# Low-rank and key projections from x times the norm's weight, scaled per token in PSUM

## The chip, the cores and the metric

One core of one Trainium2 chip runs the whole program. The metric is the device time of one execution in microseconds (us); a smaller time is better. TensorE (PE) does the matmuls, VectorE (DVE), ScalarE (ACT) and GpSimd (POOL) the elementwise work, and the DMA queues of SyncE (SP) and POOL move data.

## What is computed

A decoder block on 512 tokens of width 1024, all in float32. The part that the change touches is its beginning: a root-mean-square norm and one wide projection.

```python
def rmsnorm(x, g):
    xf = x.astype(jnp.float32)
    y = xf * lax.rsqrt(jnp.mean(xf * xf, axis=-1, keepdims=True) + NORM_EPS)
    return (y * g.astype(jnp.float32)).astype(x.dtype)
...
        h = rmsnorm(x, norm_mix_g[l])
        proj = h @ w_in[l]
        u_conv, u_rw, gate_logits = jnp.split(
            proj, [COL_CONV, COL_CONV + COL_RKV + COL_LORA], axis=-1)
...
    u = token_shift_lerp(u, mu)
    r, k, v, lw, la, lg = jnp.split(
        u, [RW_WIDTH, 2 * RW_WIDTH, 3 * RW_WIDTH,
            3 * RW_WIDTH + LORA_W, 3 * RW_WIDTH + LORA_W + LORA_A], axis=-1)
```

Of `proj`, the key columns k (512) and the low-rank columns lw, la, lg (160) are used first. Behind them come r, v, the columns of a convolution branch and 2048 gate columns, then a delta-rule recurrence, two output projections, a second norm, and an expert layer over 16384 experts that takes the larger part of the time.

## The kernel before

Channels lie on the 128 partitions and the 512 tokens along the free axis. x is loaded as `xin`, 8 chunks of 128 channels by 512 tokens; h has the same form. Every float32 projection is made of three fp32r matmuls (`mm3`, line 384): each operand is split into a high part (a rounded copy, made by ACT) and a low part (the difference, made by DVE), and high x high, high x low and low x high are summed in a PSUM bank. So h has the tiles `hH` and `hL`, a weight block has `wH` and `wL`, and the low-rank weights have `wloH` and `wloL`.

The weights of the wide projection come as blocks of 128 output channels, w0, w1 and so on. Blocks w0 to w3 give the keys, w4 to w7 r, w8 to w11 v. A block is 8 chunks x 3 = 24 matmuls of 512 columns. Raw blocks lie in four buffers (`wraw`), split ones in only two (`wH`, `wL`): block n+2 can be split when the matmuls of block n are done. ACT makes the high part in `split_h(n)` (line 1025), DVE the low part in `split_l(n)` (line 1467), and PE waits for `wl_ready` before a block.

Each engine runs a program of its own in the order written; semaphores join them. The order of the start is, on each engine:

- ACT: squares of the 8 chunks of x; the high part of the low-rank weights (line 1042); the square root of the norm (line 1045, tile `rs`); w0 and w1 split; the 8 high parts of h; then `lora_a` and `lora_b` out of PSUM, scaled (line 1056), a tanh and a sigmoid on them, and for each block its scaled copy out of PSUM into `k_in` (line 1097) and `split_h(n + 2)`.
- DVE: the sum of the squares (`grow_sum`), the low part of the low-rank weights, the reciprocal of `rs` (line 1493), then in one loop h and its low part chunk by chunk (lines 1495 to 1500), `split_l(0)`, `split_l(1)`, the token shift of both low-rank results and of each block (`lerp`, line 1505), each block's followed by `split_l(n + 2)`.
- PE: the mean of the squares over channels (`mean_square`, line 403, one float32 matmul with a matrix of 1/1024, called ms1), the low-rank projection `lora_a` (64 outputs) and `lora_b` (96 outputs), 24 matmuls each, then `units_free()` (line 376), which waits until the banks 0 to 5 are free, and blocks w0 to w11 in turn.

A bank is handed over by two semaphores: PE raises `filled`, and the last reader raises `taken`. Blocks w0, w1, ... use the banks 6 and 7 in turn, so block n waits for block n-2 to be taken.

## Time and profile before

| | us |
|---|---|
| median of 3 runs | 1812.72 |
| lowest to highest | 1811.16 to 1813.22 |
| the profiled execution | 1812.87 |
| its span in the trace | 1810.9 |

The span is what the trace covers, from the first to the last instruction; the profiled execution took 2.0 us more than that. PE is busy for 96% of the span. The stretch in which it isn't is the start, and the change lies there. The timeline, which lists instructions with their start and length in order of time, is the view to read, together with the bracket behind a row, which tells how long the engine had been idle and who ended it.

### The profile page before, as it was taken

To read this page: it belongs to the slowest core of one execution; us is meant where nothing else is said; L and a number is where in the kernel's file an instruction comes from. 1 tells how busy PE (TensorE), PEld (TensorE's weight loads), DVE (VectorE), ACT (ScalarE), POOL (GpSimd) and SP (SyncE) were. 2 spreads that over 40 slices of the span, in tenths; PEclk is the share of its full clock that TensorE was granted. 3 is DMA by queue.
4 is the path that set the end of the run, shared out by engine and by line. 5 is a ranking of instruction groups with operands and counts; after the bars stand their busy time and mean duration, and the time that the engine had idled before them with its cause. 6 is when DMAs were issued, how large, how long until landed. Compare 5 with 4: busy or idle time off the path is not lost.

```text
span 1810.9 us, 33740 instructions
## 1 busy us (share of the span) xinstructions
PE 1745.3 (96%) x11997; PEld 1542.4 (85%) x11997; DVE 1421.2 (78%) x2759; ACT 737.1 (41%) x1049; POOL 593.5 (33%) x532
## 2 busy tenths in 40 slices
PE   5989999999979999999999899999999999999998
PEld 3878888877858799999999888888888888888887
DVE  5377777846479999979998588888888888888886
ACT  4464544352232233347777233333333333333333
POOL 0000000002000166678886344443333433334430
PEclk9999999989989999999999999999999999999999
DMA  4221121116222144456666999999999999999992
GB/s 162 82 71 37 49 77 55 54 66 243 94 75 77 69 160 159 159 175 251 223 223 228 352 377 367 367 361 349 336 330 343 343 348 348 347 361 339 336 335 84
DMA packets 157823, 399.06 MB, mean 220 GB/s; under 512 B 12432, under 2 KB 78096, under 8 KB 155696
## 3 DMA queue, kind: packets, MB, share of 16 engines
q1 hardware_dynamic: 118032, 252.20, 39.8%
q0 software_dynamic: 39712, 145.77, 21.5%
q8 instruction: 54, 0.88, 0.2%
q14 instruction: 25, 0.20, 0.0%
HBM read 353.88 MB, written 44.04 MB: 220 GB/s over the span
## 4 chain that ended last, share of the span: by engine, by line
PE 54%; issue 15%; POOL 4%; DMA 2%; DVE 1%; SPq 1%; ACT 0%; POOLq 0%; ACTq 0%; DVEq 0%
PE unit L382 54%; POOL uL L2105 4%; DMA vraw<-v_tab 1%; SPq L928 0%; DMA g_dram<-ge 0%; DMA sgw<-gate_dram 0%; DVE yo L2069 0%; SPq L941 0%; DVE accs L2006 0%; ACT vH L1011 0%; DVE aL L1981 0%; DVE mb L1836 0%; DVE uL L1945 0%; DVE wL L1471 0%; ACT sqj L1011 0%
## 5 line engine op out<-in xcount | busy, mean ns | idle before, releaser
L382 PE MATMUL unit<-h2H,uH 128*128 128x384 f32 x1024 | 355.8, 347 | 11.3 <-POOL uL L2105 9.1
L382 PE MATMUL unit<-h2H,uL 128*128 128x384 f32 x1024 | 344.9, 337 | 0.0
L382 PE MATMUL unit<-h2L,uH 128*128 128x384 f32 x1024 | 344.5, 336 | 0.0
L2133 POOL DMA_INDIRECT ring<-u_tab,idx x128 | 170.7, 1333 | 230.2 <-DVE accs L2006 198.1
L382 PE MATMUL unit<-vH,aH 128*128 128x512 f32 x768 | 238.6, 392 | 5.1 <-DVE vL L1987 5.1
L382 PE MATMUL unit<-vL,aH 128*128 128x512 f32 x768 | 237.7, 391 | 0.0
L382 PE MATMUL unit<-vH,aL 128*128 128x512 f32 x768 | 237.6, 391 | 0.0
L1987 DVE TENSOR_TENSOR vL<-vraw,vH 128x1024 fp32r<-128x1024 f32 x128 | 156.6, 1224 | 88.9 <-ACT vH L1011 88.5
L2133 POOL DMA_INDIRECT ring<-v_tab,idx x128 | 141.1, 1102 | 241.0 <-DVE ring L1992 238.3
L1011 ACT ACTIVATE aH<-af 128x384 fp32r<-128x384 f32 x128 | 67.0, 524 | 366.1 <-DVE af L1976 366.1
L382 PEld LDWEIGHTS unit<-h2H,uH 128*128 128x128 f32 x1024 | 193.9, 189 | 21.5 <-POOL uL L2105 16.1
L382 PEld LDWEIGHTS unit<-h2L,uH 128*128 128x128 f32 x1024 | 193.8, 189 | 2.4
L382 PEld LDWEIGHTS unit<-h2H,uL 128*128 128x128 f32 x1024 | 193.3, 189 | 0.0
L2105 POOL TENSOR_TENSOR uL<-uraw,uH 128x1024 fp32r<-128x1024 f32 x40 | 112.0, 2801 | 191.0 <-ACT uH L1011 191.0
L1011 ACT ACTIVATE ge<-unit 128x384 f32<-128x384 f32 x128 | 62.0, 484 | 269.7 <-PE unit L382 264.4
L382 PEld LDWEIGHTS unit<-vL,aH 128*128 128x128 f32 x768 | 144.7, 188 | 31.3
L382 PEld LDWEIGHTS unit<-vH,aL 128*128 128x128 f32 x768 | 144.4, 188 | 30.8
L382 PEld LDWEIGHTS unit<-vH,aH 128*128 128x128 f32 x768 | 143.7, 188 | 31.3 <-DVE vL L1987 5.4
L2006 DVE SCALAR_TENSOR_TENSOR accs<-ring,spa,accs 128x1024 f32<-128x1024 f32 x128 | 164.2, 1283 | 4.7 <-DVE spa L1997 3.3
L2122 POOL TENSOR_SCALAR oh<-cst,e2s 128x128 f32<-128x128 f32 x192 | 148.7, 787 | 30.2 <-PE unit L382 27.7
L1992 DVE SCALAR_TENSOR_TENSOR ring<-ring,h2T 128x1024 f32<-128x1024 f32 x128 | 156.2, 1220 | 0.0
L2078 POOL DMA_DIRECT2D gate_dram<-gst x16 | 8.9, 554 | 402.9 <-ACT gst L1011 402.9
(298 smaller groups left out, 3411.4 us busy)
## 6 DMA issues: line engine op xcount, KB each, us to landing
uraw<-uT SPq DMA_DIRECT2D x128, 512.0 KB, 7.6
vraw<-v_tab SPq DMA_DIRECT2D x128, 512.0 KB
wraw<-wall SPq DMA_DIRECT2D x68, 512.0 KB, 3.7
w_dram<-wst SPq DMA_DIRECT2D x12, 2048.0 KB, 6.7
wg<-w_dram SPq DMA_DIRECT2D x32, 768.0 KB
g_dram<-ge SPq DMA_DIRECT2D x64, 192.0 KB, 1.9
gl<-g_dram SPq DMA_DIRECT2D x32, 384.0 KB
gate_dram<-gst POOLq DMA_DIRECT2D x16, 256.0 KB, 2.4
```

The lines of the kernel that those rows point to most:

```text
L382: return pe.matmul(out, lhsT, rhs, start=start, stop=stop, skip_group_check=True)
L1011: return act.activation(out, in_, f, **kw)
L1987: tt(vL[:, g, :], vraw[:, g, :], vH[:, g, :], ALU.subtract).then_inc(vl_dve, 1)
L1992: stt(ring[k][:, :], ring[k][:, :], 1.0, h2T[:, :], ALU.mult, ALU.mult, accum_out=spd[:, k:k + 1]).then_inc(row_used, 1)
L2006: stt(accs[:, :], ring[k][:, :], spa[:, k:k + 1], accs[:, :], ALU.mult, ALU.add).then_inc(row_used, 1)
L2078: pool.dma_start(gate_dram[k], gst[:, k % 2, :]).then_inc(gate_stored[k % 2], 16)
L2105: pool.tensor_tensor(uL[:, slot % 2, :, :], uraw[:, slot, :, :], uH[:, slot % 2, :, :], ALU.subtract).then_inc(ul_ready, 1)
L2122: ins = pool.tensor_scalar(oh2[:, b, k, :], C(C_IOTA), e2s[:, tok:tok + 1], None, ALU.is_equal)
L2133: pool.indirect_dma_start(out=ring[k][:, :], out_offset=None, in_=(u_tab, v_tab)[half], in_offset=bass.IndirectOffsetOnAxis(ap=idx[:, SR * ...
```

## The change

Since the norm divides a token's whole column by one number, h @ W is (x * g) @ W scaled per token. For the low-rank columns and the key blocks w0 to w3 the kernel now multiplies with `xa` = x * g and scales the result in PSUM:

- `xa` gets a high part `xaH` (ACT, a copy of `xin` scaled by the weight) and a low part `xaL` (DVE), in memory of their own. They come first on both engines, with the split of the low-rank weights behind the fifth chunk. The squares, their sum and the splits of w0 and w1 come after that.
- PE begins with the low-rank matmuls, now chunk by chunk for both outputs, then makes ms1, and then w0 to w3 from `xa`. w2 and w3 use the banks 3 and 4. `units_free()` comes behind w3, and w4 and all later blocks use h as before.
- A new DVE instruction `scale_back` multiplies a result in PSUM by `rs`. There are six: both low-rank results behind the fourth chunk of the loop that makes h, w0 behind that loop, and w1 to w3 each behind the token shift of the block ahead of it. ACT's scaled copies wait for them (`scaled`).
- `split_h(2)` and `split_l(2)` move into the loop that makes h, behind its sixth chunk; the later ones stay behind their blocks.
- On the SP queue the vectors come first, then x, the low-rank weights, `cst`, w0, and only then the other constants and w1 to w3.

```diff
@@ -119,2 +119,4 @@
     xin = at("xin", 159, [P, DC, T])
+    xaH = [at(f"xaH{k}", o, [P, DC // 2, T], F32R) for k, o in enumerate((81, 60))]
+    xaL = at("xaL", 191, [P, DC, T], F32R)
     hH = at("hH", 93, [P, DC, T], F32R)
@@ -278,3 +280,4 @@
                                           ["cst_loaded", "lora_loaded", "small_loaded", "keys_loaded"])
-        s_x = [sem(f"x{i}_loaded") for i in range(2)]
+        s_x, s_vec = [sem(f"x{i}_loaded") for i in range(2)], sem("vec_loaded")
+        xa_high, xa_split, scaled = sem("xa_high"), sem("xa_split"), sem("scaled")
         sum_grown = sem("sum_grown")
@@ -413,3 +416,14 @@
                 for c in range(DC // 2):
+                    if n == CB:
+                        pe.wait_ge(h_split, c + 1)
                     mm3(o[:, :], wH[:, n % WSPL, c, :], wL[:, n % WSPL, c, :], hH[:, c, :], hL[:, c, :], c == 0, False)
+            def key_block(n):
+                o = begin(f"w{n}", 6 - 3 * (n // 2) + n % 2)
+                pe.wait_ge(wl_ready, n + 1)
+                for c in range(DC):
+                    last = mm3(o[:, :], wH[:, n % WSPL, c, :], wL[:, n % WSPL, c, :],
+                               xaH[c // 4][:, c % 4, :], xaL[:, c, :], c == 0, c == DC - 1)
+                last.then_inc(fill_sem(f"w{n}"), 1)
@@ -418,2 +432,4 @@
                 for c in range(DC // 2, DC):
+                    if n == CB:
+                        pe.wait_ge(h_split, c + 1)
                     last = mm3(o[:, :], wH[:, n % WSPL, c, :], wL[:, n % WSPL, c, :], hH[:, c, :], hL[:, c, :],
@@ -427,14 +443,16 @@
-            pe.wait_ge(s_cst, 80)
+            pe.wait_ge(wlol_ready, 1)
+            lora = [(name, begin(name, b), lo, n) for name, b, lo, n in
+                    (("lora_a", 1, 0, LW + LA), ("lora_b", 2, LW + LA, LG))]
+            for c in range(DC):
+                pe.wait_ge(xa_split, c + 1)
+                for name, o, lo, n in lora:
+                    last = mm3(o[0:n, :], wloH[:, c, lo:lo + n], wloL[:, c, lo:lo + n],
+                               xaH[c // 4][:, c % 4, :], xaL[:, c, :], c == 0, c == DC - 1)
+                    if c == DC - 1:
+                        last.then_inc(fill_sem(name), 1)
+            pe.wait_ge(s_cst, 64)
             mean_square("ms1", 0, rs, 0)
-            pe.wait_ge(wlol_ready, 1)
-            for name, b, lo, n in (("lora_a", 1, 0, LW + LA), ("lora_b", 2, LW + LA, LG)):
-                o = begin(name, b)
-                for c in range(DC):
-                    pe.wait_ge(h_split, c + 1)
-                    last = mm3(o[0:n, :], wloH[:, c, lo:lo + n], wloL[:, c, lo:lo + n], hH[:, c, :], hL[:, c, :],
-                               c == 0, c == DC - 1)
-                last.then_inc(fill_sem(name), 1)
+            for n in range(CB):
+                key_block(n)
@@ -661,3 +679,3 @@
             pe.wait_ge(s_small, 32)
-            for n in range(W_CONV):
+            for n in range(CB, W_CONV):
                 if n == 5:
@@ -905,2 +923,3 @@
         def _(sp):
+            sp.dma_start(vec[:, :], vecs).then_inc(s_vec, 16)
             for i in range(2):
@@ -908,3 +927,5 @@
                 sp.dma_start(xin[:, half, :], xT[:, half, :]).then_inc(s_x[i], 16)
+            sp.dma_start(wlo[:, :, :], wlora).then_inc(s_lora, 16)
             sp.dma_start(cst[:, :, :], consts).then_inc(s_cst, 16)
+            sp.dma_start(wraw[:, 0, :, :], wall[0]).then_inc(w_loaded[0], 16)
             sp.dma_start(sml[:, :, :], smalls).then_inc(s_cst, 16)
@@ -912,5 +933,3 @@
             sp.dma_start(rst[:, :], reset).then_inc(s_cst, 16)
-            sp.dma_start(vec[:, :], vecs).then_inc(s_cst, 16)
-            sp.dma_start(wlo[:, :, :], wlora).then_inc(s_lora, 16)
-            for s in range(WRAW):
+            for s in range(1, WRAW):
                 sp.dma_start(wraw[:, s, :, :], wall[s]).then_inc(w_loaded[s], 16)
@@ -1034,2 +1053,3 @@
+            act.wait_ge(s_vec, 16)
             for c in range(DC):
@@ -1037,2 +1057,9 @@
                     act.wait_ge(s_x[c // (DC // 2)], 16)
+                fn(xaH[c // 4][:, c % 4, :], xin[:, c, :], ACT.Copy, scale=vc("gmix", c)).then_inc(xa_high, 1)
+                if c == DC // 2:
+                    act.wait_ge(s_lora, 16)
+                    fn(wloH[:, :, :], wlo[:, :, :], ACT.Copy).then_inc(wloh_ready, 1)
+            for c in range(DC):
+                if c == 2:
+                    split_h(0)
                 if c >= 2:
@@ -1040,10 +1067,8 @@
                 fn(sq[:, c % 2, :], xin[:, c, :], ACT.Square).then_inc(sq_ready, 1)
-            act.wait_ge(s_lora, 16)
-            fn(wloH[:, :, :], wlo[:, :, :], ACT.Copy).then_inc(wloh_ready, 1)
+            split_h(1)
             wait_filled(act, "ms1")
-            act.wait_ge(s_cst, 80)
             root(rs[:, :], "ms1", 0).then_inc(take_sem("ms1"), 1)
-            split_h(0)
-            split_h(1)
             for c in range(DC):
+                if c == 6:
+                    split_h(2)
                 act.wait_ge(h_new, c + 1)
@@ -1053,4 +1078,4 @@
-            for name, dst, n, col in (("lora_a", lwa, LW + LA, 12), ("lora_b", lgs, LG, 13)):
-                wait_filled(act, name)
+            for k, (name, dst, n, col) in enumerate((("lora_a", lwa, LW + LA, 12), ("lora_b", lgs, LG, 13))):
+                act.wait_ge(scaled, k + 1)
                 fn(dst[0:n, :], ps(name)[0:n, :], ACT.Copy, scale=omu[0:n, col:col + 1]).then_inc(lora_part, 1)
@@ -1094,6 +1119,10 @@
             for n in range(W_CONV):
-                wait_filled(act, f"w{n}")
+                if n < CB:
+                    act.wait_ge(scaled, n + 3)
+                else:
+                    wait_filled(act, f"w{n}")
                 dst = {"k": k_in, "r": r_in, "v": v_in}[KRV[n // CB]]
                 fn(dst[:, n % CB, :], ps(f"w{n}")[:, :], ACT.Copy, scale=omu[:, n:n + 1]).then_inc(lerp_part, 1)
-                split_h(n + 2)
+                if n:
+                    split_h(n + 2)
                 if n == 3:
@@ -1483,13 +1512,28 @@
+            dve.wait_ge(s_vec, 16)
+            tick(tsc(omka[:, :], vc("ka", 0, CB), -1.0, 1.0, ALU.mult, ALU.add))
+            tick(tsc(omu[:, :], vc("mu", 0, 14), -1.0, 1.0, ALU.mult, ALU.add))
+            for c in range(DC):
+                dve.wait_ge(xa_high, c + 1)
+                stt(xaL[:, c, :], xin[:, c, :], vc("gmix", c), xaH[c // 4][:, c % 4, :], ALU.mult, ALU.subtract
+                    ).then_inc(xa_split, 1)
+                if c == DC // 2:
+                    dve.wait_ge(wloh_ready, 1)
+                    tt(wloL[:, :, :], wlo[:, :, :], wloH[:, :, :], ALU.subtract).then_inc(wlol_ready, 1)
             for c in range(DC):
                 grow_sum(0, rs, sq, c)
-            dve.wait_ge(s_cst, 80)
-            tick(tsc(omka[:, :], vc("ka", 0, CB), -1.0, 1.0, ALU.mult, ALU.add))
-            tick(tsc(omu[:, :], vc("mu", 0, 14), -1.0, 1.0, ALU.mult, ALU.add))
-            dve.wait_ge(wloh_ready, 1)
-            tt(wloL[:, :, :], wlo[:, :, :], wloH[:, :, :], ALU.subtract).then_inc(wlol_ready, 1)
+                if c == 4:
+                    split_l(0)
+            split_l(1)
             wait_taken(dve, "ms1")
-            tick(dve.reciprocal(rs[:, :], rs[:, :]))
+            rs_ready = tick(dve.reciprocal(rs[:, :], rs[:, :]))
             after()
+            def scale_back(name, n):
+                wait_filled(dve, name)
+                after(rs_ready)
+                tt(ps(name)[0:n, :], ps(name)[0:n, :], rs[0:n, :], ALU.mult).then_inc(scaled, 1)
             for c in range(DC + 1):
@@ -1500,5 +1544,8 @@
                     tt(hL[:, c - 1, :], h[:, c - 1, :], hH[:, c - 1, :], ALU.subtract).then_inc(h_split, 1)
-            split_l(0)
-            split_l(1)
+                if c == 3:
+                    scale_back("lora_a", LW + LA)
+                    scale_back("lora_b", LG)
+                elif c == 6:
+                    split_l(2)
+            scale_back("w0", P)
@@ -1562,3 +1609,6 @@
                 lerp(f"w{n}", dst[:, n % CB, :], P, vc("mu", n), lerp_part, n + 1, take_sem(f"w{n}"))
-                split_l(n + 2)
+                if n:
+                    split_l(n + 2)
+                if n + 1 < CB:
+                    scale_back(f"w{n + 1}", P)
                 if n == 4:
```

PE at the start. In these rows `unit` is the PSUM bank, `rs,cst` is ms1, `xaH_73` and `xaH_74` are the two halves of `xaH`. Before:

```order
L382 MATMUL unit<-rs,cst 128x512 [waits sum_grown,cst_loaded]
L382 MATMUL unit<-hH,wloH 64x512 [waits h_split,wlol_ready]
...
L382 MATMUL unit<-hH,wH 128x512 [waits small_loaded,bank2_taken,wl_ready,bank1_taken,bank0_taken]
L382 MATMUL unit<-hL,wH 128x512
L382 MATMUL unit<-hH,wL 128x512
```

and now:

```order
L385 MATMUL unit<-xaH_73,wloH 64x512 [waits xa_split,wlol_ready]
...
L385 MATMUL unit<-rs,cst 128x512 [waits sum_grown,cst_loaded]
L385 MATMUL unit<-xaH_73,wH 128x512 [waits wl_ready]
...
L385 MATMUL unit<-hH,wH 128x512 [waits small_loaded,bank4_taken,bank6_taken,bank3_taken,wl_ready,bank2_taken,h_split,bank1_taken,bank0_taken]
```

ms1 has moved from the front to behind the 48 low-rank matmuls, and the wait for banks 0 to 5 from w0 to w4, where it now takes in w2 and w3 too.

DVE behind the reciprocal of the norm: the end of the loop that makes h, and what follows until the fourth block is split. Before:

```order
L1497 SCALAR_TENSOR_TENSOR h<-xin,vec,rs 128x512
L1500 TENSOR_TENSOR hL<-h,hH 128x512 [waits h_high] x2
L1471 TENSOR_TENSOR wL<-wraw,wH 128x1024 [waits wh_ready] x2
L1508 SCALAR_TENSOR_TENSOR lwa<-unit,vec,lwa 64x511 [waits lora_part]
L1508 SCALAR_TENSOR_TENSOR lgs<-unit,vec,lgs 96x511 [waits lora_part]
L1508 SCALAR_TENSOR_TENSOR k_in<-unit,vec,k_in 128x511 [waits lerp_part]
L1471 TENSOR_TENSOR wL<-wraw,wH 128x1024 [waits wh_ready]
L1508 SCALAR_TENSOR_TENSOR k_in<-unit,vec,k_in 128x511 [waits lerp_part]
```

and now:

```order
L1500 TENSOR_TENSOR wL<-wraw,wH 128x1024 [waits wh_ready]
L1541 SCALAR_TENSOR_TENSOR h<-xin,vec,rs 128x512
L1544 TENSOR_TENSOR hL<-h,hH 128x512 [waits h_high] x2
L1537 TENSOR_TENSOR unit<-unit,rs 128x512 [waits dve_order,bank6_filled]
L1555 SCALAR_TENSOR_TENSOR lwa<-unit,vec,lwa 64x511 [waits lora_part]
L1555 SCALAR_TENSOR_TENSOR lgs<-unit,vec,lgs 96x511 [waits lora_part]
L1555 SCALAR_TENSOR_TENSOR k_in<-unit,vec,k_in 128x511 [waits lerp_part]
L1537 TENSOR_TENSOR unit<-unit,rs 128x512 [waits dve_order,bank7_filled]
L1555 SCALAR_TENSOR_TENSOR k_in<-unit,vec,k_in 128x511 [waits lerp_part]
L1500 TENSOR_TENSOR wL<-wraw,wH 128x1024 [waits wh_ready]
```

The first `wL` row of the new order is `split_l(2)`, inside the loop; the last is `split_l(3)`, behind two token shifts of keys and the scaling of w0 and w1.

ACT in the same place, the high parts of h (`hH`), the low-rank results (`lwa`, `lgs`), the keys (`k_in`) and the splits (`wH`). Before:

```order
L1011 ACTIVATE hH<-h 128x512 [waits h_new] x8
L1011 ACTIVATE lwa<-unit,omu 64x512 [waits bank1_filled,zero_ready]
L1011 ACTIVATE lgs<-unit,omu 96x512 [waits bank2_filled]
L1011 ACT_TABLE_LOAD
L1011 ACTIVATE lwa<-lwa 32x512 [waits bank1_taken]
L1011 ACT_TABLE_LOAD
L1011 ACTIVATE lgs<-lgs 96x512 [waits bank2_taken]
L1011 ACTIVATE k_in<-unit,omu 128x512 [waits bank6_filled]
L1011 ACTIVATE wH<-wraw 128x1024 [waits bank6_filled,w2_loaded]
```

and now:

```order
L1030 ACTIVATE wH<-wraw 128x1024 [waits bank6_filled,w2_loaded]
L1030 ACTIVATE hH<-h 128x512 [waits h_new] x2
L1030 ACTIVATE lwa<-unit,omu 64x512 [waits scaled,zero_ready]
L1030 ACTIVATE lgs<-unit,omu 96x512 [waits scaled]
L1030 ACT_TABLE_LOAD
L1030 ACTIVATE lwa<-lwa 32x512 [waits bank1_taken]
L1030 ACT_TABLE_LOAD
L1030 ACTIVATE lgs<-lgs 96x512 [waits bank2_taken]
L1030 ACTIVATE k_in<-unit,omu 128x512 [waits scaled] x2
L1030 ACTIVATE wH<-wraw 128x1024 [waits bank7_filled,w3_loaded]
```

The split of w2 has moved ahead of the last two high parts of h; that of w3, the last row, stands behind both copies of keys and both table loads.

## Rows read from the trace of the kernel before

**Rows 1.** Stretches (us): length, busy PE, PEld, DVE, ACT, POOL, PE clock, DMA share, GB/s.
```profile
0.00:10.00 10.00, 0.00 (x0) 0.00 (x0) 2.94 (x6) 4.64 (x7) 0.19 (x4) 1.00 0.81 306
60.30:1810.90 1750.60, 1707.02 (x11852) 1515.99 (x11850) 1390.77 (x2720) 710.63 (x1015) 593.31 (x528) 0.98 0.62 223
```

**Rows 2.** Timeline, PE: start, length, out<-in, count, idle before and releaser.
```profile
12.95 2.05 PE L382 MATMUL unit<-rs,cst 128*128 128x512 f32 x2 [12.95 <-DVE rs L1480]
22.03 0.66 PE L382 MATMUL unit<-hH,wloH 128*64 128x512 f32 x1 [7.03 <-DVE hL L1500]
...
28.03 0.42 PE L382 MATMUL unit<-hH,wloL 128*64 128x512 f32 x1
...
36.37 0.40 PE L382 MATMUL unit<-hH,wloL 128*96 128x512 f32 x1
...
38.48 0.47 PE L382 MATMUL unit<-hH,wH 128*128 128x512 f32 x1 [1.71 <-issue]
...
60.33 0.39 PE L382 MATMUL unit<-hH,wH 128*128 128x512 f32 x1
```

**Rows 3.** Timeline, ACT and DVE up to the reciprocal's end.
```profile
6.14 1.75 ACT L1011 ACTIVATE sq<-xin 128x512 f32<-128x512 f32 x3 [4.12 <-DMA xin<-xT]
...
13.05 1.27 ACT L1011 ACTIVATE wloH<-wlo 128x1280 fp32r<-128x1280 f32 x1 [1.18 <-DMA wlo<-wlora]
...
14.35 1.49 DVE L1490 TENSOR_TENSOR wloL<-wlo,wloH 128x1280 fp32r<-128x1280 f32 x1 [1.39 <-ACT wloH L1011]
15.63 0.69 ACT L1011 ACTIVATE rs<-unit,vec 128x512 f32<-128x512 f32 x1
...
16.35 3.35 DVE L1493 RECIPROCAL rs<-rs 128x512 f32<-128x512 f32 x1 [0.51 <-ACT rs L1011]
```

**Rows 4.** Groups by line, 0 to 500 us: float32 matmuls of 512 columns, busy us, mean ns.
```profile
L382 PE MATMUL unit<-cy,cst 128*128 128x512 f32 x8 | 3.7, 605 | 0.0
```

**Rows 5.** Timeline, DVE and ACT: the loop that makes h, and the splits behind it.
```profile
19.74 1.42 DVE L1497 SCALAR_TENSOR_TENSOR h<-xin,vec,rs 128x512 f32<-128x512 f32 x2
...
28.11 0.75 DVE L1497 SCALAR_TENSOR_TENSOR h<-xin,vec,rs 128x512 f32<-128x512 f32 x1
...
28.90 0.63 ACT L1011 ACTIVATE hH<-h 128x512 fp32r<-128x512 f32 x1 [0.63 <-DVE h L1497]
...
30.17 2.35 DVE L1471 TENSOR_TENSOR wL<-wraw,wH 128x1024 fp32r<-128x1024 f32 x2
```

**Rows 6.** Timeline, DVE: an operation that reads PSUM.
```profile
115.22 0.68 DVE L1615 TENSOR_TENSOR lt<-unit,sml 128x512 f32<-128x512 f32 x1
```

**Rows 7.** Timeline, ACT and DVE: low-rank results, first keys, split of w2.
```profile
36.81 0.68 ACT L1011 ACTIVATE lgs<-unit,omu 96x512 f32<-96x512 f32 x1 [4.82 <-PE unit L382]
37.51 1.28 ACT L1011 ACT_TABLE_LOAD   x1
...
40.75 0.63 ACT L1011 ACTIVATE lgs<-lgs 96x512 f32<-96x512 f32 x1
44.20 0.69 ACT L1011 ACTIVATE k_in<-unit,omu 128x512 f32<-128x512 f32 x1 [2.83 <-PE unit L382]
...
45.88 1.23 DVE L1471 TENSOR_TENSOR wL<-wraw,wH 128x1024 fp32r<-128x1024 f32 x1 [0.20 <-ACT wH L1011]
```

**Rows 8.** Timeline, PE: small matmuls of the key norms, then block w5.
```profile
65.77 3.86 PE L382 MATMUL unit<-sel,sqk 128*128 128x8 f32 x32
69.48 0.77 PE L382 MATMUL unit<-hH,wH 128*128 128x512 f32 x1
...
72.54 0.39 PE L382 MATMUL unit<-hL,wH 128*128 128x512 f32 x1
```

**Rows 9.** Stretches of 2 us around them, columns as in rows 1.
```profile
70.00:72.00 2.00, 2.00 (x6) 1.56 (x5) 0.00 (x0) 0.00 (x0) 0.00 (x0) 0.50 0.80 258
```

**Rows 10.** Timeline, PE and ACT: the next wait of PE, and the work that leads to it.
```profile
119.26 1.28 ACT L1011 ACT_TABLE_LOAD   x1 [5.82 <-PE unit L382]
...
135.10 1.13 PE L382 MATMUL unit<-bh,nkt 64*64 64x64 f32 x32 [4.58 <-DVE r_in L1555]
```

## The prediction

> **What bounds the kernel now.** I read the stretches first. Behind 60.3 us PE is busy for 1707.0 of 1750.6 us [rows 1], so whatever moves the start of that part moves the end. It begins with block w4, at 60.33 [rows 2], and from w4 on the change leaves every instruction as it was. The question is therefore one number: when does w4 start? The timeline of PE shows what precedes it now. PE is idle up to 12.95, makes ms1, is idle 7.03 us more until the first chunk of h is split at 22.03, does the low-rank matmuls until about 36.8, waits 1.71 us for their banks, and then runs w0 to w3 without a gap from 38.48 [rows 2]. So some 22 us of the first 38 are waits for the norm and for h. The change lets PE begin without the norm. What then matters is the chain on ACT and DVE that the norm still feeds, because w2, w3 and w4 hang on it.
>
> Two prices of a matmul of 512 columns serve throughout. At full speed it is (60.33 - 38.48) / 96 = 0.228 us [rows 2]. From 22.03 to 28.03 fourteen of them took 6.0 us, 0.43 each [rows 2]: half speed, after a long idle stretch. The same is seen behind the small matmuls of the key norms: from 69.48 to 72.54 seven took 3.06 us [rows 8], with a granted clock of 0.50, the 1.2 GHz level [rows 9]. So a cold start costs 6.0 - 14 x 0.228 = 2.8 us in the one case and 3.06 - 7 x 0.228 = 1.5 us in the other.
>
> **Part 1: when PE starts.** Now the low-rank weights land at 13.05, when their split begins [rows 3]. About 1.0 MB (cst, two small tables and the reset mask) goes behind them in the queue; at 306 GB/s with the DMA engines 0.81 busy, thus up to 378 [rows 1], that is 2.6 to 3.3 us earlier, less 0.3 for the 0.1 MB of vectors put in front of x: 10.1 to 10.7. ACT has x at 6.14 [rows 3], now 6.4; its table load of 1.28 us waits for x in the new order, and five copies at about 0.6 (three squares took 1.75 [rows 3]) end at 10.7. So transfer and copies arrive together. The split of these weights takes 1.30 us to the start of its low part and 1.49 more [rows 3]: ready at 13.5, PE starts at 13.7. All `xaL` chunks are there in time: PE takes six matmuls a chunk, 1.4 us at the least, DVE 0.7.
>
> Low-rank: 48 x 0.228 = 10.9 us plus a cold start of 1.5 to 2.8, of which I take 2.1: end at 26.7 (26.1 to 27.4). The sum of squares and the splits of w0 and w1 on ACT and DVE, 8 squares, 8 sums and four splits, are done by 25, in the cover of this; if they were later, ms1 would be later by as much. ms1 is a float32 matmul: 3.7 us for 8 pieces [rows 4], two pieces here, about 1.0 at full speed (2.05 now [rows 2]). Filled at 27.8. w0 and w1 follow at 27.7 and end at 38.6.
>
> **Part 2: the split of w2.** The square root starts at 27.9. From its start to the first chunk of h is 19.74 - 15.63 = 4.11 us [rows 3, 5], so h begins at 32.0. The loop reaches the place of `split_l(2)` after 28.11 - 19.74 = 8.37 us [rows 5], plus two `scale_back` of the low-rank results. No row has that operation; an operation of the same size that reads PSUM takes 0.68 [rows 6]. Writing PSUM too could cost nothing or as much again; I take 0.6 each, since they overlap a little. `split_l(2)` starts at 41.6 and takes 1.2 [rows 5]: w2 can start at 42.9. **PE idles 4.3 us** behind w1.
>
> **Part 3: the split of w3.** This is the long wait. Behind `split_l(2)` the last h chunk starts at 42.75; its high part starts 0.79 later and takes 0.63 [rows 5], so ACT is free at 44.2. Then, in order: the copy of `lora_a` 0.65, and from the start of the copy of `lora_b` to the end of the sigmoid 40.75 + 0.63 - 36.81 = 4.57 [rows 7], with two table loads in it: 49.4. Copy of w0's keys, 0.73 until DVE can take it (as from root to reciprocal, 16.35 - 15.63 [rows 3]): 50.1. Token shift of w0 and `scale_back` of w1, 0.65 each: 51.5 with the handover. Then as now from a key copy to the low part of the next block, 45.88 - 44.20 = 1.68, and 1.23 for it [rows 7]: 54.4. w3 starts at 54.6. w2 has ended between 48.4 and 51.2, at full speed or cold, and that difference is hidden. **PE idles 3.4 to 6.2 us.**
>
> **Part 4: w4.** w3 needs 24 x 0.228 = 5.45 us plus a cold start p of 0 to 2.8. `units_free()` now waits for w3: `scale_back` 0.1 + 0.7, copy 0.73, token shift 0.75, handover 0.2 make 2.5 us. w4 starts at 54.6 + 5.45 + 2.5 + p = 62.5 + p. For p I take 1.4: a wait of this length has both outcomes near it (1.71 us idle at 36.8 left the speed as it was [rows 2]; the 4.58 at 130.5 and what led up to it stand for the other side [rows 10]), and 1.5 is the smaller of the two cold starts.
>
> **Sum.** 63.9 against 60.33, thus 3.6 us later. What it saves, the start at 13.7 instead of 22.03, is given back in three waits of 4.3, 3.4 to 6.2 and 2.5 us. The profiled execution took 1812.87, its span plus 2.0, and the median is 1812.72: 1812.7 + 3.6 = 1816.3. Everything later shifts by the same amount. I checked the first wait behind w4 for slack: PE idles 4.58 us up to 135.10, but the ACT work that leads to it itself waited 5.82 us for PE at 119.26 [rows 10], so it moves along.
>
> A rule of the skill speaks against the change. The two table loads, which the new order puts on PE's path, take 1.28 us with nothing behind them: from the first load's start to the sigmoid is 3.24 us, two loads and the tanh [rows 7]. The Trainium skill, page ScalarE: Activation LUTs, section What ACT_TABLE_LOAD costs, puts a drain of about 1.38 us on top of each switch. By that rule the sum would be about 2.8 us more, estimated from that page; the rows have no room for it.
>
> **The rivals.**
>
> (a) *A kind clock, not slower.* The low-rank matmuls start warm after a short stretch (1.5), w2's lateness leaves PE idle so briefly that w3 starts at full speed (p = 0), and the slow stretch behind the key norms [rows 8] falls elsewhere, a gain of up to 1.5. From 63.9: -0.6 - 1.4 - 1.5, thus w4's start in effect at 60.4 and 1812.8. It decides at p: with p under 0.5 and a short cold start the change is level. For it: the 1.71 us wait cost nothing. Against: both waits are twice that and more.
>
> (b) *An unkind clock, slower.* The long cold start (2.8), p = 2.8, and one more short cold start at w4 behind its wait of 2.5: +0.7 + 1.4 + 1.5 on the sum, 1819.9.
>
> (c) *Slack behind w4.* If the waits behind it were for work that the new order finishes earlier (the low-rank results), 3.6 us would be taken up in part: 1812.7 to 1815. Against it stands [rows 10].
>
> (d) *The chain is dearer than its rows.* `scale_back` in PSUM at twice the price, six of them with four on the path (+2.7), or table loads with a pause behind them: 1819 to 1821. The table-load rule above gives 1819.1 as its own result; I give that 3%.
>
> (e) *The change does not do what it says*: PE does not start before 22, because the low-rank weights land late. Then ms1 is 8 us later and so is all behind it: 1824. Only a queue that ignores its order could do that.
>
> **How the numbers follow.** The sum as worked out, 1814.5 to 1818.5, has 0.58; (a) 0.14; (b) 0.12; (c) 0.06; (d) 0.08; (e) 0.02. The likeliest case gives 1816.3. The range reaches from inside (a) to (b) and the start of (d): 1812.5 to 1820.5. Of this kernel 0.2%, or 3.6 us, is about what can be told from no change. The forecast lies on that line: half of the main case is above it, with (b), (d), (e), which makes 0.50 slower; 0.47 within; 0.03 faster, since nothing that I see takes w4 3.6 us ahead of 60.33. The Trainium skill, page TensorE: Matmul & The Clock Gate, Part 1, says that the number of slow matmuls at a start differs from run to run of one kernel; no run here shows that yet, and it would be a reason for a spread of the size of (a) and (b).
>
> **What would show each step right or wrong.** The first low-rank matmul near 13.7 (part 1); ms1 behind them near 26.7; the first matmul of w2 near 42.9 with 4.3 us of idle time, released by DVE's `wL` (part 2); the first of w3 near 54.6, also released by `wL` (part 3); w4 near 64 with about 2.5 us idle (part 4); the length of w3 tells p. Behind w4 the stretches should be as before, 1750.6 us. The prediction is wrong if w2 or w3 starts without a wait, or if the part behind w4 changes its length by more than 1.5 us.

## The result

| | before | changed |
|---|---|---|
| median, 14 runs each | 1810.16 us | 1815.77 us |
| the profiled execution of the changed kernel | | 1817.64 us, span 1815.7 |
| ratio of the times, changed to before | | 1.0028, 95% interval 1.0020 to 1.0037 |

The change makes the kernel slower by 0.28%, about 5.1 us; 3.6 us were forecast, and a time inside 1812.5 to 1820.5 us. One of the 14 runs of the changed kernel took 1952.60 us at a mean granted clock of 0.842; it isn't in the ratio, and the median of the other 13 is 1815.38 us.

Where the time is, is told by one cut. Stretches of the changed kernel, from the start to w4 and from w4 to the end (columns as in [rows 1]):

```profile
0.00:65.65 65.65, 40.56 (x146) 29.28 (x147) 40.33 (x55) 32.79 (x45) 0.19 (x4) 0.92 0.39 136
65.65:1815.70 1750.05, 1707.45 (x11851) 1515.20 (x11851) 1390.73 (x2719) 708.82 (x1013) 593.87 (x528) 0.99 0.62 223
```

Behind w4 it is 1750.05 us, 1750.60 before [rows 1]. So in these two traces the whole difference lies ahead of w4, which starts at 65.65 instead of 60.33: 5.3 us, and the medians differ by about as much.

The timeline of PE shows the shape (as [rows 2]; `xaH,wH` are blocks from xa, `hH,wH` is w4):

```profile
14.12 0.69 PE L385 MATMUL unit<-xaH,wloH 128*64 128x512 f32 x1 [14.12 <-DVE wloL L1522]
...
18.44 0.63 PE L385 MATMUL unit<-xaL,wloH 128*96 128x512 f32 x1
18.87 0.48 PE L385 MATMUL unit<-xaH,wloL 128*96 128x512 f32 x1
...
27.50 1.02 PE L385 MATMUL unit<-rs,cst 128*128 128x512 f32 x2
...
43.52 0.79 PE L385 MATMUL unit<-xaH,wH 128*128 128x512 f32 x1 [4.09 <-DVE wL L1500]
...
50.19 0.39 PE L385 MATMUL unit<-xaH,wL 128*128 128x512 f32 x1
54.77 0.80 PE L385 MATMUL unit<-xaH,wH 128*128 128x512 f32 x1 [4.19 <-DVE wL L1500]
55.36 0.63 PE L385 MATMUL unit<-xaL,wH 128*128 128x512 f32 x1
...
62.57 0.39 PE L385 MATMUL unit<-xaH,wL 128*128 128x512 f32 x1
65.65 0.47 PE L385 MATMUL unit<-hH,wH 128*128 128x512 f32 x1 [2.70 <-issue]
```

The first low-rank matmul starts 7.9 us earlier than before (14.12 for 22.03). Behind that PE idles three times: 4.09 us for the low part of w2, 4.19 for that of w3, 2.70 at the banks ahead of w4. The lengths tell the second half of the loss: matmuls of 0.63 us are at half speed, those of 0.39 at full speed (the next one starts 0.43 and 0.23 us later). w3 goes from 54.77 to 62.8, 8.0 us for 5.45. The clock in stretches of 2 us within w4 falls as well:

```profile
66.00:68.00 2.00, 2.00 (x8) 1.60 (x7) 0.62 (x1) 1.81 (x3) 0.00 (x0) 0.71 0.20 37
68.00:70.00 2.00, 2.00 (x6) 1.52 (x6) 0.00 (x0) 0.00 (x0) 0.00 (x0) 0.50 0.60 225
```

w4 ran for 7.2 us, though its first matmuls were at full speed: the granted clock fell to 0.50, the 1.2 GHz level, after PE had begun again.

Why w3 is so late is read on ACT and DVE (compare [rows 7]):

```profile
44.70 0.67 ACT L1030 ACTIVATE lwa<-unit,omu 64x512 f32<-64x512 f32 x1
45.27 0.67 ACT L1030 ACTIVATE lgs<-unit,omu 96x512 f32<-96x512 f32 x1
45.95 1.28 ACT L1030 ACT_TABLE_LOAD   x1
47.25 0.63 ACT L1030 ACTIVATE lwa<-lwa 32x512 f32<-32x512 f32 x1
47.90 1.28 ACT L1030 ACT_TABLE_LOAD   x1
49.19 0.63 ACT L1030 ACTIVATE lgs<-lgs 96x512 f32<-96x512 f32 x1
49.73 0.67 ACT L1030 ACTIVATE k_in<-unit,omu 128x512 f32<-128x512 f32 x1
```

```profile
45.43 0.69 DVE L1537 TENSOR_TENSOR unit<-unit,rs 128x512 f32<-128x512 f32 x1
46.03 0.73 DVE L1555 SCALAR_TENSOR_TENSOR lwa<-unit,vec,lwa 64x511 f32<-64x511 f32 x1
46.69 0.73 DVE L1555 SCALAR_TENSOR_TENSOR lgs<-unit,vec,lgs 96x511 f32<-96x511 f32 x1
50.43 0.75 DVE L1555 SCALAR_TENSOR_TENSOR k_in<-unit,vec,k_in 128x511 f32<-128x511 f32 x1 [3.01 <-ACT k_in L1030]
51.10 0.69 DVE L1537 TENSOR_TENSOR unit<-unit,rs 128x512 f32<-128x512 f32 x1
52.54 0.75 DVE L1555 SCALAR_TENSOR_TENSOR k_in<-unit,vec,k_in 128x511 f32<-128x511 f32 x1 [0.75 <-ACT k_in L1030]
53.49 1.23 DVE L1500 TENSOR_TENSOR wL<-wraw,wH 128x1024 fp32r<-128x1024 f32 x1 [0.20 <-ACT wH L1030]
```

w0's keys were scaled in PSUM from 46.1 on (first DVE row), but ACT copies them at 49.73, behind the tanh, the sigmoid and two table loads. DVE waits 3.01 us for that. Only then come w1's keys, and behind them the split of w3, at PE's disposal from 54.7.

### The profile page after: what moved, and what is told of

Same layout as the page of the kernel before. It is cut to its first block, busy times and chain, and to the rows that moved or that the text cites. A ratio compares the mean times of both kernels' runs of the same rounds, so it can differ in the third digit from the quotient of the medians.

```text
span 1815.7 us, 33768 instructions
## 1 busy us (share of the span) xinstructions
PE 1748.0 (96%) x11997; PEld 1544.5 (85%) x11997; DVE 1431.1 (79%) x2773; ACT 741.6 (41%) x1057; POOL 594.1 (33%) x532
## 4 chain that ended last, share of the span: by engine, by line
PE 54%; issue 15%; POOL 4%; DMA 2%; DVE 1%; SPq 1%; ACT 0%; POOLq 0%; ACTq 0%; DVEq 0%
PE unit L385 54%; POOL uL L2155 4%; DMA vraw<-v_tab 1%; SPq L947 0%; DMA g_dram<-ge 0%; DMA sgw<-gate_dram 0%; DVE yo L2119 0%; SPq L960 0%; DVE accs L2056 0%; ACT vH L1030 0%; DVE aL L2031 0%; DVE mb L1886 0%; DVE uL L1995 0%; DVE wL L1500 0%; ACT sqj L1030 0%
## 5 line engine op out<-in xcount | busy, mean ns | idle before, releaser
L2183 POOL DMA_INDIRECT ring<-u_tab,idx x128 | 174.6, 1364 | 225.2 <-DVE accs L2056 192.4
```

The lines of the kernel that those rows point to most:

```text
L2183: pool.indirect_dma_start(out=ring[k][:, :], out_offset=None, in_=(u_tab, v_tab)[half], in_offset=bass.IndirectOffsetOnAxis(ap=idx[:, SR * ...
```

## The experiments

The theory: the time follows the start of w4, and that start is set by a chain (ms1, root, h, ACT's queue, splits, banks) plus PE's clock. Each of the first four kernels is the changed kernel with one link of it taken out. One table holds them all; "w4" is the start of its first matmul in the trace, "behind w4" the rest of the span, the ratio is to the kernel before on the same chip, and the last column is the ratio's distance from 1, times 1810.

| kernel | w4 | behind w4 | ratio (95% interval) | us against before |
|---|---|---|---|---|
| before | 60.33 | 1750.6 | | |
| changed | 65.65 | 1750.0 | 1.0028 (1.0020 to 1.0037) | +5.1 |
| e1, banks waited for later | 59.49 | 1748.1 | 1.0003 (0.9992 to 1.0014) | +0.5 |
| e2, tanh and sigmoid later | 58.49 | 1748.8 | 1.0009 (0.9995 to 1.0023) | +1.6 |
| e3, matmuls of no use in the waits | 64.33 | 1746.9 | 1.0015 (1.0002 to 1.0028) | +2.7 |
| e4, ms1 earlier | 60.23 | 1746.5 | 1.0010 (1.0000 to 1.0020) | +1.8 |
| e5, low-rank part alone | 68.45 | 1749.2 | 1.0051 (1.0036 to 1.0066) | +9.2 |
| e6, own tiles for w2 and w3 | 60.81 | 1750.2 | 1.0023 (1.0013 to 1.0034) | +4.2 |
| c1 = e1 + e2 + e4 | 54.10 | 1749.7 | 0.9954 (0.9940 to 0.9967) | -8.3 |
| c2 = c1 + e6 | 49.76 | 1749.2 | 0.9950 (0.9937 to 0.9964) | -9.1 |

Two things limit what this table can tell. First, "less than the changed kernel" below is a difference of two ratios, each with its interval; put together (the half-widths added in squares, an estimate) they leave 2.4 to 3.1 us on either side. Second, w4 is read from one execution, and that one lies up to 3.7 us from its kernel's median: 2.7 us above it for the kernel before (1812.87 against 1810.16), 2.3 above for the changed one (1817.64 against 1815.38), 2.0 below for e2, 3.7 below for e4. The time against before and the shift of w4 agree to within 4 us in all nine kernels, with the largest gaps at e6 (3.7) and e2 (3.4); so the theory holds in the main and is not shown to better than that.

### e1: the wait for the banks

```diff
-            units_free()
             pe.wait_ge(s_small, 32)
             for n in range(CB, W_CONV):
                 if n == 5:
+                    units_free()
                     key_norms()
```

> The changed kernel, with the wait for banks 0 to 5 moved from ahead of w4 to ahead of the key norms, the first that needs them; w4 itself uses bank 6. Theory (the time follows the start of w4 and its clock): in the changed kernel PE idles 2.70 us from the end of w3 (62.8) to w4 (65.65), and w4 is then partly at half speed, 7.2 us long for 5.45. Now w4 starts near 62.9, warm: 2.8 + 1.7 = 4.5 us less than the changed kernel, which is level with the kernel before within 1 us. Rival (what follows w4, its key norms and the low-rank work, waits for the same ACT and DVE work anyway): w4 starts early, but the key norms start at 72.8 as they do now, and nothing is gained.

Measured: 4.5 us less than the changed kernel by the ratios (2.0 to 7.0 with both intervals), level with before. w4 follows w3 without a gap:

```profile
53.92 0.50 PE L385 MATMUL unit<-xaH,wH 128*128 128x512 f32 x1 [2.69 <-DVE wL L1500]
...
59.27 0.39 PE L385 MATMUL unit<-xaH,wL 128*128 128x512 f32 x1
59.49 0.39 PE L385 MATMUL unit<-hH,wH 128*128 128x512 f32 x1
...
64.94 3.63 PE L385 MATMUL unit<-sel,sqk 128*128 128x8 f32 x32
```

The key norms start at 64.94, not at 72.8, so the rival falls. The gain is the one expected, but in the trace w4 starts even 6.2 us earlier, and not all of that is the edit's. The edit gives 2.9 us; the start of the trace (w0 at 27.12, not 27.96) gives 0.8. And in this trace w2 ran cold for longer (13 slow matmuls for 6), which cost nothing since w3 was not yet split, but made the idle time ahead of w3 2.69 us instead of 4.19, and w3 ran at full speed, 2.6 us less. That part is the clock, not the edit.

### e2: tanh and sigmoid off ACT's way

```diff
-            wait_taken(act, "lora_a")
-            fn(lwa[0:LW, :], lwa[0:LW, :], ACT.Tanh).then_inc(lora_ready, 1)
-            wait_taken(act, "lora_b")
-            fn(lgs[:, :], lgs[:, :], ACT.Sigmoid).then_inc(lora_ready, 1)
...
+                elif n == 4:
+                    wait_taken(act, "lora_a")
+                    fn(lwa[0:LW, :], lwa[0:LW, :], ACT.Tanh).then_inc(lora_ready, 1)
+                    wait_taken(act, "lora_b")
+                    fn(lgs[:, :], lgs[:, :], ACT.Sigmoid).then_inc(lora_ready, 1)
                 elif n == 5:
```

> The changed kernel, with the tanh and the sigmoid of the low-rank results (and their two table loads) moved on ACT behind block w4's copy; they are first needed at w6. Theory (the split of w3 hangs on ACT's queue): ACT can copy w0's keys at 46.2 instead of 49.7, DVE then sets the pace with two token shifts of the low-rank results, the low part of w3 ends at 51.7 instead of 54.7, w3 starts near 51.8 after an idle time of 1.3 us and so at full speed, and w4 starts near 59.9 instead of 65.65: 5.8 to 7.5 us less than the changed kernel, 1 to 2 us less than before. Rival (DVE's own work, scaling in PSUM above all, holds the chain): w3 moves by less than 1 us and the time by less than 1.5.

ACT and DVE in this kernel:

```profile
43.67 0.67 ACT L1030 ACTIVATE lgs<-unit,omu 96x512 f32<-96x512 f32 x1
44.56 0.69 ACT L1030 ACTIVATE k_in<-unit,omu 128x512 f32<-128x512 f32 x1 [0.22 <-DVE unit L1538]
```

```profile
48.80 1.23 DVE L1501 TENSOR_TENSOR wL<-wraw,wH 128x1024 fp32r<-128x1024 f32 x1 [0.20 <-ACT wH L1030]
```

and PE, the first matmuls of w3 and w4:

```profile
50.08 0.50 PE L385 MATMUL unit<-xaH,wH 128*128 128x512 f32 x1
...
58.49 0.47 PE L385 MATMUL unit<-hH,wH 128*128 128x512 f32 x1 [2.67 <-issue]
```

From the copy of `lora_b` to the keys of w0 it is 0.9 us instead of 4.5, and the low part of w3 is ready at 50.0, 8.1 us behind the start of w2 (41.92) where it took 11.2. w3 follows w2 without a wait (w2 itself had eleven slow matmuls), w4 starts at 58.49, after much the same wait at the banks (2.67). In the trace w4 is 7.2 us earlier, but 1.6 us of that are there before any of the edit acts: ms1 starts at 25.92, not 27.50, since PE began 0.6 us sooner and six matmuls were slow at the start instead of eleven. By the ratios the gain on the changed kernel is 3.4 us (0.4 to 6.4), less than the 5.8 expected. The chain is as the theory says; how much of it reaches the time is less certain, since its interval reaches from -0.9 to +4.2 us against before and the forecast of 1 to 2 us faster lies at or beyond its lower end. The rival falls by its first half, since w3 starts 4.7 us earlier where it allowed 1; its gain of less than 1.5 us is not excluded by the times.

### e3: keeping PE busy in its waits

```diff
+            def keep_busy(k):
+                for _ in range(k):
+                    mm(bank[5][:, :], xaH[0][:, 0, 0:P], xaH[0][:, 0, :])
+
             for n in range(CB):
+                if n >= 2:
+                    keep_busy((16, 16)[n - 2])
                 key_block(n)
+            keep_busy(8)
```

> The changed kernel, with matmuls of no use (xa with itself, into bank 5, which nobody reads) in PE's waits: 16 ahead of w2, 16 ahead of w3, 8 behind w3. Starts of w2 and w3 should stay at 43.5 and 54.8, as ACT and DVE set them. Theory (cold starts cost 2.6 us in w3 and 1.7 in w4): w3 takes 5.5 us instead of 8.0, w4 starts near 63.1 and takes 5.5 instead of 7.2: 4.3 us less than the changed kernel, 0.5 to 1 over before. Rival (the clock would have paid its slow stretch later anyway, at the key norms, as it did in the kernel before): w4 starts at 63.1 but the gain at the end is 2.5 us or less.

```profile
54.26 0.51 PE L385 MATMUL unit<-xaH,wH 128*128 128x512 f32 x1 [1.85 <-DVE wL L1507]
...
55.31 0.51 PE L385 MATMUL unit<-xaL,wH 128*128 128x512 f32 x1
55.62 0.63 PE L385 MATMUL unit<-xaH,wL 128*128 128x512 f32 x1
```

w2 began at full speed, at 43.01. The 16 matmuls ahead of w3 ended at 52.4, 1.85 us too early, and w3 started fast but then fell to half speed for seven matmuls. w4 was at full speed. So w4 starts 1.3 us earlier, and the ratios differ by 2.4 us, half of what was expected and not clear of no gain at all (-0.4 to 5.2). The kernel did not keep w3 at full speed, so it is no clean test of what the cold starts cost; both theories stay open. In the trace w4 took 5.5 us instead of 7.2, but this kernel paid more behind the key norms: there eleven matmuls ran slowly, in the changed kernel and in the kernel before seven. An idle time of 1.7 us left the clock as it was in the kernel before [rows 2], one of 1.85 us was followed by a fall here.

### e4: ms1 earlier

```diff
             for c in range(DC):
+                if c == 5:
+                    pe.wait_ge(s_cst, 64)
+                    mean_square("ms1", 0, rs, 0)
                 pe.wait_ge(xa_split, c + 1)
...
-            pe.wait_ge(s_cst, 64)
-            mean_square("ms1", 0, rs, 0)
```

> The changed kernel, with the mean of the squares (ms1) moved on PE from behind the eighth chunk of the low-rank matmuls to ahead of the sixth: the sum of squares is there at 22.9, the sixth chunk starts at 23.3, the place of ms1 in the changed kernel is 27.5. Theory (everything from the root on is a chain behind ms1): root at 24.4 instead of 28.6, w2 at 39.5 right behind w1, w3 at 50.7 after 5.7 us idle and cold, w4 near 61.3: 4 us less than the changed kernel, about 1 over before. Rival (the chain is held by ACT and DVE work that does not hang on ms1): the root is 4 us earlier but w3 moves by less than 2.

```profile
24.28 0.69 ACT L1031 ACTIVATE rs<-unit,vec 128x512 f32<-128x512 f32 x1 [0.43 <-PE unit L385]
```

```profile
39.24 0.50 PE L385 MATMUL unit<-xaH,wH 128*128 128x512 f32 x1
...
50.49 0.80 PE L385 MATMUL unit<-xaH,wH 128*128 128x512 f32 x1 [5.51 <-DVE wL L1501]
60.23 0.76 PE L385 MATMUL unit<-hH,wH 128*128 128x512 f32 x1 [2.67 <-issue]
```

Root at 24.28, w2 right behind w1, w3 at 50.49 after 5.51 us idle: each within 0.3 us of what was written down. w4 is 1.1 us earlier than expected, since w3 was slow for six matmuls only, and the time 3.3 us below that of the changed kernel (0.9 to 5.7). The rival falls: w3 moved by 4.3 us.

PE's order is only the smaller part of the norm's lateness. The root starts at 24.28 here, and at 15.63 in the kernel before [rows 3]. These 8.7 us are left to ACT and DVE, where the splits of xa, of the low-rank weights and of w0 stand ahead of or among the squares and their sum. In the changed kernel the last three sums are:

```profile
20.63 2.28 DVE L1509 TENSOR_TENSOR rs<-rs,sq 128x512 f32<-128x512 f32 x3
```

so the sum is there at 22.9, where ms1 could start at 12.95 before [rows 2]. No kernel here makes the squares first, so what that order would give, and what it would cost at PE's start, is not known.

### e5: the low-rank part alone

```diff
-            for n in range(CB):
-                key_block(n)
...
-            for n in range(CB, W_CONV):
+            for n in range(W_CONV):
...
-                    act.wait_ge(scaled, n + 3)
+                wait_filled(act, f"w{n}")
...
-                if n + 1 < CB:
-                    scale_back(f"w{n + 1}", P)
```

(and `split_h(2)`, `split_l(2)` back behind w0, `scale_back("w0", P)` gone.)

> The changed kernel with its key part undone: only the low-rank columns are made from xa and scaled in PSUM; w0 to w3 are made from h, in the banks 6 and 7, with their splits behind them, as in the kernel before. Theory (the norm is late because ms1 stands behind the low-rank matmuls, and everything that needs h waits for it): the loop that makes h still ends near 44.3, the low-rank results are taken near 46.3, w0 starts near 46.5, cold after some 18 us idle, and w4 near 70 against 65.65 in the changed kernel: 3 to 4 us slower than that, 8 to 9 slower than before. Rival (the key part, with its four scalings and its late splits, is what costs): it is faster than the changed kernel.

```profile
45.02 0.76 PE L385 MATMUL unit<-hH,wH 128*128 128x512 f32 x1 [17.36 <-DVE lwa L1544]
...
68.45 0.39 PE L385 MATMUL unit<-hH,wH 128*128 128x512 f32 x1
```

PE waits 17.36 us for h and the low-rank results; w4 starts 2.8 us later than in the changed kernel, and the time is 4.2 us above it (1.1 to 7.3). This kernel ran only four times, within 1819.28 to 1821.18 us. So the key part is not what costs: it wins back a part of what the late norm takes. The loss comes with the low-rank part, which puts work ahead of the norm, on PE ahead of ms1 (e4) and on ACT and DVE ahead of the squares.

### e6: tiles of their own for the splits of w2 and w3

```diff
+    wX = {2: (at("w2H", 44, [P, DC, P], F32R), at("w2L", 48, [P, DC, P], F32R)),
+          3: (at("w3H", 181, [P, DC, P], F32R), at("w3L", 185, [P, DC, P], F32R))}
...
-                if c == 6:
+                if c == 3:
                     split_h(2)
+                elif c == 5:
+                    split_h(3)
...
-                elif c == 6:
+                elif c == 4:
                     split_l(2)
+                elif c == 6:
+                    split_l(3)
...
-                if n:
-                    split_h(n + 2)
+                if n in (1, 2):
+                    split_h(n + 3)
+                elif n >= 4:
+                    split_h(n + 2)
```

> The changed kernel, with tiles of their own for the split weights of w2 and w3, in memory that is free at that time, so that both can be split inside the loop that makes h; the splits of w4 and w5 move forward to behind w1 and w2. Theory: w0 to w3 run without a gap from 28.5 to 50.3; but w4 still waits until w3 is scaled, copied and shifted, and that hangs on ACT's queue with the tanh and the sigmoid: w4 near 62, cold, against 65.65. So the two long waits turn into one of 11 us, and only 3.5 us are gained on the changed kernel, 1.5 slower than before. Rival (the late splits are the whole loss): w4 near 53 and 10 us gained.

```profile
39.88 0.50 PE L393 MATMUL unit<-xaH,w2H 128*128 128x512 f32 x1 [1.56 <-DVE w2L L1514]
60.81 0.77 PE L393 MATMUL unit<-hH,wH 128*128 128x512 f32 x1 [9.75 <-issue]
```

```profile
49.22 0.63 ACT L1038 ACTIVATE lgs<-lgs 96x512 f32<-96x512 f32 x1
49.76 0.67 ACT L1038 ACTIVATE k_in<-unit,omu 128x512 f32<-128x512 f32 x1
```

The two waits for splits shrink to 1.56 us (none was expected), and one of 9.75 stands ahead of w4. ACT comes to the keys of w0 at 49.76, as in the changed kernel (49.73), and three more blocks of keys have to be scaled, copied and shifted behind it. The time is only 0.9 us below that of the changed kernel by the ratios (-1.5 to 3.3), less than the 3.5 expected and not clear of no gain, where the trace has w4 4.8 us earlier. Slow matmuls explain little of that gap: nine in w4 and seven behind the key norms, where the changed kernel had seven and seven. Of the 4.8 us, 1.1 were there at ms1 (26.40 for 27.50), and the two traces lie 1.2 us below and 2.3 us above their kernels' medians. The rest stays open. Late splits are thus not the whole loss; they are one of two ends of the same chain.

### c1 and c2: the edits together

> Three of the single edits together: the wait for the banks at the key norms, tanh and sigmoid behind w4's copy, ms1 ahead of the sixth low-rank chunk. Theory (their gains lie one behind the other on one chain and add up, less what the cold starts take): root 24.4, w2 at 39.4, w3 near 47.5, w4 right behind it near 53 against 60.33 in the kernel before: 7 us faster than before, ratio 0.996. Rival (the gains overlap): w4 at 57 or later, 3 us or less.

> The same three edits, and the early splits of w2 and w3 as well. Theory: PE runs from 13.9 to the key norms without a wait, w4 starts at 49.5 to 50, 10.5 us ahead of the kernel before, and the key norms start near 55.3: 10 to 11 us faster than before, ratio 0.994, and 15 faster than the changed kernel. Rival (the stages behind w4 then wait for ACT and DVE, which have not been freed by as much): half of it.

```profile
22.63 1.10 PE L385 MATMUL unit<-rs,cst 128*128 128x512 f32 x2 [0.22 <-DVE rs L1511]
...
46.91 0.50 PE L385 MATMUL unit<-xaH,wH 128*128 128x512 f32 x1 [2.37 <-DVE wL L1502]
...
54.10 0.39 PE L385 MATMUL unit<-hH,wH 128*128 128x512 f32 x1
```

That is c1: behind ms1 one wait is left, 2.37 us for w3, with seven slow matmuls in that block. In c2 it is gone too:

```profile
13.96 0.69 PE L393 MATMUL unit<-xaH,wloH 128*64 128x512 f32 x1 [13.96 <-DVE wloL L1538]
...
49.76 0.39 PE L393 MATMUL unit<-hH,wH 128*128 128x512 f32 x1
...
55.73 2.48 PE L393 MATMUL unit<-sel,sqk 128*128 128x8 f32 x21 [0.38 <-ACT sqk L1039]
```

Both are faster than the kernel before and the changed one: c1 by 0.46%, c2 by 0.50%, against 0.4 and 0.6 expected. The gains of e1, e2 and e4 do add up within what can be told: 4.5, 3.4 and 3.3 make 11.2 us, and c1 is 13.4 us below the changed kernel. From c1 to c2 w4 starts 4.3 us earlier in the traces, but the times differ by less than their intervals, so the forecast of 10 to 11 us for c2 is neither reached nor excluded (9.1, interval 6.5 to 11.4); c2 is the fastest by its median, 1801.73 us, without c1 being shown slower.

## The prediction, step by step

The forecast was 3.6 us slower; it is 5.1. The time itself came closer, 1816.3 forecast and 1815.77 measured, but that is luck: the forecast added its 3.6 to a median of three runs, 1812.72, and 14 runs of the same kernel have 1810.16. By its own steps, in the trace of the changed kernel:

| step | predicted | measured |
|---|---|---|
| PE starts | 13.7 | 14.12 |
| ms1 starts | 26.7 | 27.50 |
| root, first chunk of h | 27.9, 32.0 | 28.56, 32.67 |
| w2 starts, idle before | 42.9, 4.3 | 43.52, 4.09 |
| sigmoid ends | 49.4 | 49.8 |
| w3 starts, idle before | 54.6, 3.4 to 6.2 | 54.77, 4.19 |
| cold start in w3 (p) | 1.4 | 2.6 |
| w4 starts, idle before | 63.9, 2.5 | 65.65, 2.70 |
| behind w4 | 1750.6 | 1750.0 |

**Part 1 held**, 0.4 us late, since x was there at 6.9, not 6.4 (timeline of ACT):

```profile
6.91 1.28 ACT L1030 ACT_TABLE_LOAD   x1 [6.91 <-DMA xin<-xT]
```

The low-rank matmuls had eleven at half speed, so a cold start of 2.2 us where 2.1 was taken, and 0.2 us more went into their pitch. **Part 2 held**: `scale_back`, for which no row stood, takes 0.68 to 0.70 us with 0.6 from one to the next, as the row that reads PSUM did [rows 6]; writing PSUM as well costs nothing that can be seen. **Part 3 held**: from the root to w3 it is 26.2 us, 26.7 were summed, because its delays were rows of the same instructions. **Part 4 is where the size was off**: p was taken as 1.4 and was 8.03 - 5.46 = 2.6 us, eleven slow matmuls and the parts of one at either end. That is inside its bounds of 0 to 2.8, and the row leaned on, 1.71 us idle without effect, was too short a wait to tell of one of 4.19.

Rival (a), the kind clock, would have needed p under 0.5. Rival (b) foresaw cold starts in w3 and in w4, and both came: w4 was slow for seven matmuls, 1.7 us. It still did not come to 7 us, since the stretch behind w4, with that loss in it, is no longer than before. From the end of w4 on it is even 2.2 us shorter (1742.9 for 1745.1), and 1.8 of this is in the small matmuls of the convolution's variance, 32 of one column, in the kernel before and in the changed one:

```profile
374.62 5.57 PE L382 MATMUL unit<-cst,csq 128*128 128x1 f32 x32
```

```profile
380.55 3.73 PE L385 MATMUL unit<-cst,csq 128*128 128x1 f32 x32
```

The granted clock was 0.65 over the first (374.62 to 380.05) and 1.00 over the second (380.55 to 384.14). The change can't be what made it: these 32 took 3.73 us in the traces of changed, e1, e3 and e4, and 5.38 to 5.57 in the other six. So 1.8 us of luck in this one place hid what w4's cold start cost, a term that the sum had put at nothing.

**Rival (d)**, the table loads: from the start of the first to the sigmoid it is 49.19 - 45.95 = 3.24 us, two loads of 1.28 and a tanh of 0.63. The drain of about 1.38 us that the Trainium skill (ScalarE: Activation LUTs, section What ACT_TABLE_LOAD costs) adds to each is not there in this trace, nor in the kernel before, where the same pair takes 3.24 us too [rows 7]; the measurement decides. **Rival (c)** fell: the wait that stood at 135.10 before is 4.58 us long in the changed kernel too, up to 142.15. **Rival (e)** fell with the first row.

## To carry to other kernels

When work that needs no norm is put ahead of the norm on an in-order engine, the norm comes later by whatever of that work outlasts the norm's own input (ms1 at 27.50 for a sum ready at 22.9 here), and everything that needs it moves too: put the one small instruction that starts the longest chain as early as its input allows, in the midst of the filler. What stands ahead of that instruction counts as well: here the squares behind the splits on ACT and DVE made the norm later than PE's order did. Then follow each queue behind it: here a tanh and a sigmoid that nobody needed for 30 us, a wait for banks that the next block did not use, and two buffers for splits each held the chain in turn, and the kernel before was beaten only when several were gone. A saving at the start is worth about what the first block of the steady part starts earlier (to within 4 us here), however much sooner PE begins.

## What the runs showed of the hardware

- Nine of the ten kernels begin with the same low-rank matmuls, after 13.5 to 14.2 us without PE. In their traces the number of slow ones was 11, 10, 6, 8, 12, 9, 8, 7 and 9, and in the kernel before, where ms1 stands ahead, 14. A cold start there cost 1.5 us (e2, 12.44 us for 48 matmuls) to 2.8 us (before): a range and no constant. The Trainium skill (TensorE: Matmul & The Clock Gate, Part 1) says that the number of slow matmuls differs from run to run of one kernel; the traces agree in that kernels with the same start differ, but no kernel was traced twice.
- The profile's clock column does not show these first slow matmuls. It reads 1.00 from 14.00 to 27.50 us in the changed kernel, where eleven matmuls took 0.43 us each. They are found by their lengths.
- Not expected was that the clock also falls after PE has resumed: in w4 of the changed kernel, four matmuls after the 2.70 us wait, in e3's w3, about 1.3 us into the block and behind a wait of 1.85 us, and in c1's w3 behind 2.37 us. In e4 a wait of 2.67 us was followed by seven slow matmuls at once. But waits of 1.56 (e6), 1.71 (before), 2.67 (e2) and 2.69 us (e1) were followed by full speed. So below 3 us both happen, and a forecast should carry both.
- The clock also falls without any idle time: behind the small matmuls of the key norms (128x8, 3.86 us of them in the kernel before) some 7 to 13 matmuls of 512 columns were slow in eight of the ten traces, and none in e5 and c1.
- A slow stretch in a block that ends before its successor is ready costs nothing: in e1 w2 had 13 slow matmuls where the changed kernel had six, and the wait behind it was shorter by as much (2.69 us for 4.19).
- The stretch behind w4, the same matmuls in all ten kernels, took 1746.5 to 1750.6 us. A single trace is good to some 4 us, and differences of that size need the medians. In the kernel before, most of the spread goes along with PE's clock: of 31 runs beside e1 to e4, the three with a mean granted clock of 0.985 took 1813.5 us on average, the twelve with 0.987 1810.2, the eight with 0.988 1808.1 (correlation -0.9). In the changed kernel and those made from it the tie is looser, and what else makes their spread stays open.
